# RWKV-7 scan: the identity products of the inversion give way to an in-place mask by VectorE in PSUM

## What is computed

```python
def step(S, inp):
    r_t, w_t, k_t, v_t, kk_t, a_t = inp
    sa = jnp.einsum('bhij,bhj->bhi', S, -kk_t)
    S = (S * w_t[:, :, None, :] + sa[..., None] * (kk_t * a_t)[:, :, None, :]
         + v_t[..., None] * k_t[:, :, None, :])
    y = jnp.einsum('bhij,bhj->bhi', S, r_t)
    return S, y
```

## Time and profile before

| what | value |
|---|---|
| median of 3 runs | 3842.46 us |
| the profiled execution, its own time | 3841.41 us |
| its span, from first to last record | 3839.6 us |
| mean granted TensorE clock | 0.963 of full |
| the scan phase, first to last record of its matmuls | about 1650 to 2065 us |

### The profile page before, as it was taken

One profiled execution on the slowest core, in us unless ns is written; L12 is line 12 of the kernel. 1 busy time (PEld: TensorE's weight loads), 2 busy tenths in 40 slices (PEclk: granted clock), 3 DMA queues, 4 the chain that ended last, 5 costly groups with the idle time before them and its releaser, 6 DMA issues. The chain is left out here.

```text
span 3839.6 us, 65729 instructions
## 1 busy us (share of the span) xinstructions
PE 3534.6 (92%) x27224; PEld 3001.1 (78%) x27224; DVE 1886.0 (49%) x2785; ACT 1018.6 (27%) x1612; POOL 180.7 (5%) x336
## 2 busy tenths in 40 slices
PE   8999999999799992989998997978979999999997
PEld 7888888887677881979996676767858888888885
DVE  5444444544556305767776425113164445444546
ACT  2111111110434214456666513122041111111112
POOL 0000000000000000522220000000000000000000
PEclk9999999999899996989999999989989999999998
DMA  3100100100236312043333320010001000100101
GB/s 119 46 33 33 49 33 33 39 32 12 96 93 155 127 70 87 1 124 89 97 98 101 133 100 11 33 45 28 33 28 50 33 33 34 48 33 33 49 6 55
DMA packets 86020, 225.60 MB, mean 59 GB/s; under 512 B 6737, under 2 KB 53457, under 8 KB 79825
## 3 DMA queue, kind: packets, MB, share of 16 engines
q1 hardware_dynamic: 81808, 210.91, 16.5%
q10 hardware_dynamic: 4032, 12.06, 0.8%
HBM read 176.07 MB, written 46.87 MB: 58 GB/s over the span
## 5 line engine op out<-in xcount | busy, mean ns | idle before, releaser
L289 DVE TENSOR_TENSOR main_acc<-main_acc,ffn_psum 128x512 f32<-128x512 f32 (+1 forms) x1056 | 617.7, 598 | 852.3 <-PE ffn_psum L205 851.7
L194 PE MATMUL ffn_psum<-x_xh,ffn_wi_h 128*128 128x512 f32 (+1 forms) x2112 | 525.7, 357 | 30.0 <-DVE ffn_wi_l L278 17.9
L194 PE MATMUL ffn_psum<-x_xl,ffn_wi_h 128*128 128x512 f32 (+1 forms) x2112 | 525.5, 357 | 0.0
L194 PE MATMUL ffn_psum<-x_xh,ffn_wi_l 128*128 128x512 f32 (+1 forms) x2112 | 525.1, 357 | 0.0
L194 PEld LDWEIGHTS ffn_psum<-x_xh,ffn_wi_h 128*128 128x128 f32 x2112 | 372.9, 188 | 98.0 <-DVE ffn_wi_l L278 18.3
L194 PEld LDWEIGHTS ffn_psum<-x_xl,ffn_wi_h 128*128 128x128 f32 x2112 | 349.9, 188 | 61.3
L194 PEld LDWEIGHTS ffn_psum<-x_xh,ffn_wi_l 128*128 128x128 f32 x2112 | 349.9, 188 | 60.6
L205 PE MATMUL ffn_psum<-ffn_hid_h,ffn_wo_h 128*128 128x512 f32 (+1 forms) x1056 | 380.5, 360 | 12.5 <-DVE ffn_hid_l L297 10.0
L205 PE MATMUL ffn_psum<-ffn_hid_h,ffn_wo_l 128*128 128x512 f32 (+1 forms) x1056 | 377.7, 358 | 0.0
L205 PE MATMUL ffn_psum<-ffn_hid_l,ffn_wo_h 128*128 128x512 f32 (+1 forms) x1056 | 376.7, 357 | 0.0
L249 ACT CAST ffn_hid_h<-ffn_hid 128x1280 fp32r<-128x1280 f32 x44 | 55.6, 1264 | 1066.9 <-DVE ffn_hid L295 1066.9
(11 more groups left out here) (294 smaller groups left out, 5274.5 us busy)
## 6 DMA issues: line engine op xcount, KB each, us to landing
ffn_w_raw_in<-ffn_w_in_dram SPq DMA_DIRECT2D x44, 1024.0 KB, 5.2
rws_pack<-pack SPq DMA_DIRECT2D x160, 225.0 KB, 3.0
ffn_w_raw_out<-ffn_w_out_dram SPq DMA_DIRECT2D x44, 512.0 KB, 3.5
mixin_w_raw<-mix_w_in_dram SPq DMA_DIRECT2D x27, 512.0 KB, 3.5
pack<-mixin_pack SPq DMA_DIRECT2D x4, 2580.0 KB, 15.8
fin_raw<-ca_w_kv_dram SPq DMA_DIRECT2D x16, 512.0 KB, 3.6
pack<-mixin_pack SPq DMA_DIRECT2D x4, 1920.0 KB, 12.4
proj<-mixin_low ACTq DMA_DIRECT2D x12, 640.0 KB, 3.0
```

The costliest lines, as they stand in the source:

```text
L194: mm = nc.tensor.matmul(ps[:, at + c * BANK:at + c * BANK + tn], w[:, slot, cols], x[:, k, t0:t0 + tn], start=(k == 0 and j == 0), stop=(k ...
L289: nc.vector.tensor_tensor(acc[:, o, t0:t0 + tn], acc[:, o, t0:t0 + tn], ps[:, at:at + tn], ALU.add).then_inc(added, 1)
```

## The change

The identity products at level 0 are gone, and with them the left-half layout. R stays where `score_b` has put it (the first 64 of each 128 columns, `raw_r`). VectorE multiplies it there by the triangular mask, in place in PSUM, after level 0's cut and transpose; a new semaphore pair `seeded` tells TensorE. All levels, the last one and ScalarE's copies then use `raw_r`. The flip's product goes to the second 64 columns of each q, so it waits for `br_set`. In `score_b` only q = 0 has `start=True`, so that the later products of the levels add to what lies in the bank.

```diff
-        br_set, kr_set = each("br_set"), each("kr_set")
+        br_set, kr_set, seeded = each("br_set"), each("kr_set"), each("seeded")
...
-        flip_bank = lambda i: bank(i)[:, 4 * C:6 * C].rearrange("p (q t) -> p q t", t=C // 2)
+        flip_bank = lambda i: pairs(i)[:, :, 1, part(0)]
         LOW = LEVELS - 1
+        raw_r = lambda i: pairs(i)[:, :, 0]
...
-                            mm = nc.tensor.matmul(bank(RL[d])[own(s), q * P:(q + 1) * P], b[d][own(s), q], flat[own(s), q], start=True, stop=True)
+                            mm = nc.tensor.matmul(bank(RL[d])[own(s), q * P:(q + 1) * P], b[d][own(s), q], flat[own(s), q],
+                                                  start=(q == 0), stop=True, skip_group_check=True)
...
                     if level == 0:
                         pe.wait_ge(br_set[d], m + 1)
+                        pe.wait_ge(seeded[d], m + 1)
                         pe.wait_ge(n_set[d], LOW * m + 1)
-                        for s in HEADS:
-                            nc.tensor.matmul(left(RL[d])[own(s)], stack_ident[own(s)], now_r[own(s)], start=True, stop=True)
...
-                            mm = nc.tensor.matmul(left(RL[d])[own(s), q], n_t[d][own(s), q], now_r[own(s), q],
+                            mm = nc.tensor.matmul(raw_r(RL[d])[own(s), q], n_t[d][own(s), q], now_r[own(s), q],
                                                   start=False, stop=True, skip_group_check=True)
...
             def flip(m, d):
                 pe.wait_ge(r_set[d], LOW * (m + 1))
+                pe.wait_ge(br_set[d], m + 1)
...
-                        mm = nc.tensor.matmul(left(RL[d])[quadrant(s, d), q, part(1 - d)], n_last[d][quadrant(s, 1 - d), q],
+                        mm = nc.tensor.matmul(raw_r(RL[d])[quadrant(s, d), q, part(1 - d)], n_last[d][quadrant(s, 1 - d), q],
...
-                    nc.scalar.copy(br[d][m % 2][:, :, 0], left(RL[d])).then_inc(r_set[d], 1)
+                    nc.scalar.copy(br[d][m % 2][:, :, 0], raw_r(RL[d])).then_inc(r_set[d], 1)
...
-                    nc.scalar.copy(x_t[d][:], left(RL[d])).then_inc(x_set[d], 1)
+                    nc.scalar.copy(x_t[d][:], raw_r(RL[d])).then_inc(x_set[d], 1)
...
                     nc.vector.tensor_tensor(br[d][m % 2][:], pairs(RL[d]), each_q(both_of("kr_mask", d)), ALU.mult).then_inc(br_set[d], 1)
                     lower(m, 0, d)
+                    dve.wait_ge(n_set[d], LOW * m + 1)
+                    dve.wait_ge(br_set[d], m + 1)
+                    nc.vector.tensor_tensor(raw_r(RL[d]), raw_r(RL[d]), each_q(both_of("kr_mask", d)[:, 0]), ALU.mult).then_inc(seeded[d], 1)
```

More of the change, by code:

```diff
@@ L1633, in lower @@
                     dve.wait_ge(raised[d], LOW * m + level)
-                now_r = left(RL[d]) if level else pairs(RL[d])[:, :, 0]
-                nc.vector.tensor_tensor(n_sb[d][:], now_r, each_q(mask("level", d, level)), ALU.mult).then_inc(n_set[d], 1)
+                nc.vector.tensor_tensor(n_sb[d][:], raw_r(RL[d]), each_q(mask("level", d, level)), ALU.mult).then_inc(n_set[d], 1)
                 dve.wait_ge(n_set[d], LOW * m + level + 1)
```

## The result

| what | before | with the change |
|---|---|---|
| median, runs taken side by side | 3844.97 us (7 runs, 3842.03 to 3851.24) | 3855.43 us (7 runs, 3851.73 to 3862.01) |
| ratio | | 1.0027, 95% interval 1.0015 to 1.0038 |
| profiled execution, its own time | 3841.41 us | 3857.25 us |
| its span | 3839.6 us | 3855.5 us |

The kernel became slower by about 10.5 us.

A forecast was written before the change was run, and what follows sets the result against it. VectorE's stream up to level 1's cut was taken as the bound. Removal at nothing plus 19 x 0.67 = 12.7 us on 3841.41 made 3854.1, and 1.05 for the median gave 3855.2; range 3845 to 3862.

The forecast's parts named there:

- VectorE is the later one, by 0.12 us: At level 1's cut, VectorE is ready 5.50 us after the round's start, TensorE's level 0 at 5.38 or so.
- a single odd round: One round where a memset replaced a product, so VectorE came early and waited 0.20 us for TensorE, until 5.38.
- the prediction's own chain to level 2: Level 2's weights wait for ScalarE's copies, behind four exponentials and a copy that waits for VectorE's cut of level 1.
- The removal, priced at nothing: Four identity matmuls a round fewer on TensorE at level 0, 0.86 us of its stream, taken as worth nothing.
- The cover of 0.43 and 0.86 us: TensorE time of one direction's identity pair and of a round's four, hidden by VectorE's stream up to level 1's cut.
- The seeds: Two added in-place masks a round on VectorE before level 1's cut, 0.33 us each, 0.67 a round.
- The upper end, 0.45: Rival of dearer seeds: each in-place mask costs the 0.45 us pitch, 0.90 a round, 3859.6 us; chance 0.17.
- The path behind them: From the in-place masks through level 1's cut and ScalarE's chain: cut 0.67 us later, level 2 0.67 later.
- the slip arrives whole: All 0.67 us a round reaches level 2, with 0.3 us of margin; 12.7 us over rounds 1 to 19.
- the late gaps: TensorE gaps in a round's last quarter without a visible wait; their change was put at zero, plus or minus 3 us.
- the rival on TensorE's slack: TensorE's pause before level 1 lets instruction supply catch up, halving 14.7 us: 3847.8; chance 0.20, with a partly hidden slip.
- The 14.7 us: Mean round over shortest round, 0.82 us each, in all; said to come mostly with gaps where TensorE waits for nothing visible.

The follow-up runs named there:

- no_seed: The changed kernel without VectorE's two in-place masks and TensorE's wait for them, scan masks and state zeroed; 3845.97 us, 0.9996 of the kernel before.
- both_again: The kernel before, identity products kept, with the two in-place masks added and TensorE's level 0 waiting for them; 3853.46 us, 1.0021 of the kernel before.
- after_k_late: The changed kernel with VectorE's two masks of k moved behind level 4; 3835.79 us, 0.9986 of the kernel before.
- before_k_late: The kernel before with VectorE's two masks of k moved behind level 4; 3839.97 us, 0.9991 of the kernel before.
- double_seed: The changed kernel with each in-place mask done twice, the second waiting for the first's semaphore; 3879.41 us, 1.0085 of the kernel before.

## Why the prediction was right

**The bound.** "VectorE is the later one, by 0.12 us" is shown from both sides: with VectorE's load reduced the cut comes at 5.38, with TensorE's load reduced it stays at 5.50. It rested on a single odd round, and was read at the cut of direction 0. At direction 1's cut, from which the prediction's own chain to level 2 starts, the margin is 0.04 (6.32 against 6.28). The conclusion is the same, but the two streams were nearly level.

**The removal, priced at nothing.** Shown by no_seed and by both_again. The cover of 0.43 and 0.86 us was VectorE's stream; with the cover gone, in after_k_late, the shortest round is 0.53 shorter than in before_k_late, not 0.86: level 2 still waits for ScalarE's chain (0.23 us), and this hangs on VectorE's cut of direction 1, which came only some 0.45 earlier.

**The seeds.** Sum: 0.33 each by the pitch of the nearest rows; measured 0.31, and 0.66 a round, because two instructions right behind a seed let their successor start 0.02 later each: the b mask of d = 1 (0.60 instead of 0.58) and the state's sum (0.90 instead of 0.88). The upper end, 0.45, was the price of waiting for one's own semaphore, and double_seed shows it where it belongs: the second seed starts 0.43 to 0.44 behind the first. The sentence of the Trainium skill that the prediction goes by ("VectorE: DVE Perf Modes", section "The DRAIN you can't avoid") would make the next instruction wait for the full 0.40, and the trace again disagrees. But the prediction left out how that paragraph ends: a next operation that is not held starts earlier. With that the trace agrees, 0.31 at a length of 0.40, so the skill read whole doesn't contradict it.

**The path behind them.** The cut at 6.16 (6.17 forecast), TensorE's pause 1.14 (1 to 1.4), level 2 at 9.47 (9.5), the shortest round 20.03 (20.0). The walk through VectorE, ScalarE and TensorE held link by link.

**The sum, and where it was lucky.** The forecast was 3855.2 and the median 3855.43. But two terms were off and cancelled, which is luck: the time before was 3842.46 over three runs and 3844.97 over seven, and the slip that arrived was 10.5 us there and about 8 over all six comparisons, not 12.7. The step that did not hold is the last one, "the slip arrives whole", with the late gaps put "at zero, plus or minus 3 us": over many runs a third of the slip is missing, which is the direction of the rival on TensorE's slack, whose price (half of 14.7 us) was too large; the cause stays open. The 14.7 us themselves were also misread as coming "mostly" with gaps. The gaps of "issue" in these rounds of the kernel before add up to 6.5 us. Another 4 or so are work: in rounds 3 to 10 TensorE turns v rows (L1400) ahead of solve, which starts 0.50 later there (17.81 after the round's start in round 4, 17.31 in round 1), while the shortest round has none:

```profile
1754.64 1.15 PE L1400 MATMUL rws_psum<-rws_consts,rws_pack 64*64 64x64 f32 x32
```

**The chances.** The forecast lay 1.2 us beyond the 0.3% line and gave slower 0.56; the measured ratio lies just below that line with an interval over both sides, and by the mean over all series the change lies within it. So the side that the prediction held for likelier was missed by little; it had given the other 0.37.

## What to carry to other kernels

Busy shares told the opposite of what a round told: TensorE at 97% of a stretch was the engine that arrived first, if by no more than 0.04 to 0.12 us. Before work is moved from one engine to another, find at the meeting point which stream arrives last, and by how much; the odd round, in which one stream was early by accident, gives that number free of charge. And a removal that is worth nothing may become worth something (here 0.5 us in an undisturbed round) once work with a later deadline (here the masks of k) is moved off the stream that covered it.

## What the runs showed of the hardware

- VectorE multiplied 128x256 f32 in place in PSUM in 401 ns, about the same as out of PSUM into SBUF (406 ns), and matmuls with `start=False` then added to what it had written, where an earlier product with the flags as in `score_b` had been.
- In double_seed TensorE paused 1.74 to 2.08 us ahead of level 1 in 18 rounds. In 11 of them the granted clock was then 0.50 for a stretch (1799.57 to 1802.98 in round 6) in which TensorE was busy, and the flips came 0.8 to 1.3 us later; in 7, as after the 2.08 us of round 5, it stayed at 1.00. Pauses of 1.14 us in the changed kernel were followed by no fall between 1700 and 2000. So a slip on another engine can cost more than its length.
- TensorE's late gaps go with its instruction queue: 87 of 87 gaps above 0.3 us, in ten profiles, end 2.2 to 3.1 us after the start of a 16 KB transfer of that queue.
- Executions of one kernel here differ by several microseconds: 35 runs of the kernel before, in one series, went from 3835.55 to 3848.81. A forecast against a median of three runs carries, by my estimate from this spread, some 2 to 3 us of that.
